# Mixture of experts in blocks of tokens: the incomplete block of an expert as its last item instead of its first

## What is computed

```python
logits = (xt @ w_router + b_router).astype(jnp.float32)
top_val, top_idx = lax.top_k(logits, TOP_K)          # TOP_K = 4, 32 experts
...
def expert_block(args):                              # blocks of 128 tokens of one expert
    xblk, e = args
    gate = xblk @ w_gate[e] + b_gate[e]
    up = xblk @ w_up[e] + b_up[e]
    gate = jnp.minimum(gate, SWIGLU_LIMIT)
    up = jnp.clip(up, -SWIGLU_LIMIT, SWIGLU_LIMIT)
    h = (up + 1.0) * gate * jax.nn.sigmoid(SWIGLU_ALPHA * gate)
    return h @ w_down[e] + b_down[e]
...
y = segment_sum(yb * row_w[:, None], row_tok)        # weighted sum over a token's four experts
```

## Time and profile before

| | us |
|---|---|
| median of three runs | 2398.84 (2397.83 to 2398.97) |
| the profiled execution | 2394.5 |
| its span, first to last instruction | 2392.6 |
| TensorE busy in the span | 2221.9 |
| start of the first G | 807.22 |
| end of the last D | 2345.9 |

### The profile page before, as it was taken

The page is one execution under the profiler, slowest core; times in us unless marked ns, Lnnn a source line. Parts: engine busy times, 40 slices in busy tenths (PEclk is TensorE's granted clock), DMA queues, the critical chain, the costliest instruction groups (busy, mean ns, idle before and its releaser), DMA issues.

```text
span 2392.6 us, 57077 instructions
## 1 busy us (share of the span) xinstructions
PE 2221.9 (93%) x21767; PEld 1176.8 (49%) x21768; DVE 1043.4 (44%) x1664; ACT 668.5 (28%) x1414; POOL 376.6 (16%) x491
## 2 busy tenths in 40 slices
PE   5999999998996599999999999999998999999982
PEld 3485765867454244545445454444443444444441
DVE  4154547445346344434434443443353444433334
ACT  5111222233344332222322222322232222222222
POOL 5000000000014212111111121111122112211111
PEclk9999999999997699999999999999999999999996
DMA  9112011126205294967979788888887897888864
GB/s 302 35 36 72 26 33 48 31 67 246 93 36 202 90 373 127 360 211 279 338 250 344 251 313 314 287 305 287 286 328 272 303 340 271 309 291 337 322 216 157
DMA packets 187702, 525.54 MB, mean 220 GB/s; under 512 B 20330, under 2 KB 68066, under 8 KB 187490
## 3 DMA queue, kind: packets, MB, share of 16 engines
q1 hardware_dynamic: 133874, 338.86, 37.7%
q10 hardware_dynamic: 36240, 134.29, 14.4%
q0 software_dynamic: 17536, 51.69, 9.6%
HBM read 486.21 MB, written 38.57 MB: 219 GB/s over the span
## 4 chain that ended last, share of the span: by engine, by line
PE 85%; DMA 6%; DVE 4%; issue 1%; ACT 1%; POOL 1%; ACTq 0%; SPq 0%; POOLq 0%; DVEq 0%
PE ps L1753 40%; PE ps L1786 19%; PE ps L1536 6%; PE ps L1637 5%; PE ps L1532 5%; DMA w_gu_e<-in_w_up_dram 4%; PE ps L1542 2%; PE ps L1593 2%; PE ps L1539 2%; PE ps L1615 1%; PE ps L1656 1%; PE ps L1508 1%; DMA w_down_e<-in_w_down_dram 1%; DVE box L1107 0%; DVE y_all L1460 0%
## 5 line engine op out<-in xcount | busy, mean ns | idle before, releaser
L1753 PE MATMUL ps<-w_gu_e,xT 128*32 128x512 f32 x9216 | 1007.7, 595 | 34.3 <-DVEq L1418 16.6
L1753 PEld LDWEIGHTS ps<-w_gu_e,xT 128*32 128x32 f32 x9216 | 355.9, 110 | 667.4 <-issue 667.1
L1786 PE MATMUL ps<-w_down_e,hT 128*32 128x256 f32 x9216 | 508.7, 380 | 13.4 <-ACT yrow L932 8.4
L1786 PEld LDWEIGHTS ps<-w_down_e,hT 128*32 128x32 f32 x9216 | 351.3, 110 | 181.8 <-issue 40.8
L1383 DVE STREAM_TRANSPOSE gu_t<-ps 128x1024 f32<-128x1024 f32 x94 | 111.9, 1229 | 639.4 <-PE ps L1753 639.4
L914 ACT ACTIVATE xT<-xr,fm 128x128 f32<-128x128 f32 x392 | 184.1, 490 | 569.0 <-PE ps L1753 544.6
L1369 DVE TENSOR_SCALAR yrow<-ps,slot_tab 32x256 f32<-32x256 f32 x376 | 181.3, 482 | 259.0 <-PE ps L1786 167.9
L932 ACT ACTIVATE yrow<-ps,slot_tab 32x256 f32<-32x256 f32 x384 | 179.4, 467 | 352.2 <-issue 235.9
L655 POOL DMA_INDIRECT xg<-xn_rows,idx_g x196 | 197.4, 1007 | 85.4 <-issue 47.6
L649 POOL TENSOR_TENSOR idx_g<-slot_tab,base_row 128x4 int32<-128x4 int32 x49 | 9.2, 189 | 1101.6 <-DVE xr L1405 1087.5
L1536 PE MATMUL ps<-hxT,w_ring 128*128 128x512 f32 (+1 forms) x384 | 142.5, 529 | 3.7 <-ACT hxT L802 3.7
(11 more groups left out here) (301 smaller groups left out, 1515.2 us busy)
## 6 DMA issues: line engine op xcount, KB each, us to landing
w_gu_e<-in_w_gate_dram SPq DMA_DIRECT2D x256, 512.0 KB, 10.7
w_gu_e<-in_w_up_dram SPq DMA_DIRECT2D x256, 512.0 KB, 11.6
w_down_e<-in_w_down_dram ACTq DMA_DIRECT2D x124, 1024.0 KB, 9.2
w_ring<-in_w_ada_dram SPq DMA_DIRECT2D x17, 1024.0 KB, 5.2
w_ring<-in_w_in_dram SPq DMA_DIRECT2D x20, 512.0 KB, 5.2
w_first<-in_w_ada_dram SPq DMA_DIRECT2D x7, 1024.0 KB, 12.2
x_all<-in_x_dram SPq DMA_DIRECT2D x2, 2048.0 KB, 10.6
w_out<-in_w_out_dram SPq DMA_DIRECT2D x8, 512.0 KB, 8.6
```

The source lines that it names most:

```text
L1753: last = T.matmul(ps[j * GROUP:(j + 1) * GROUP, g, :].rearrange("p (w b f) -> p w b f", w=2, f=GROUP), xT[:, k, g * GROUP:(g + 1) * GROUP] ...
L1786: last = T.matmul(ps[j * GROUP:(j + 1) * GROUP, 4 + g // 2, g % 2 * QUARTER:(g % 2 + 1) * QUARTER], hT[:, g, k, :], w_dn[:, k, j * QUARTER ...
```

## The change

Item j of an expert is now block j, and so its last item is the incomplete one. The mark `first_it[:, 0]` is set where the item's number plus one equals the number of blocks; column 0 of `of_it` stays as it is; the number of empty groups counts for the marked item only, as before.

```diff
             link(V.tensor_scalar(of_it[:, 0:1], of_it[:, 0:1], -1.0, item, ALU.mult, ALU.add))
-            link(V.tensor_scalar(first_it[:, 0:1], of_it[:, 0:1], 0.0, None, ALU.is_equal))
-            link(V.tensor_tensor(of_it[:, 1:3], of_it[:, 1:3], first_it[:, 0:1].to_broadcast([P, 2]), ALU.mult))
-            link(V.scalar_tensor_tensor(out=of_it[:, 0:1], in0=of_it[:, 0:1], scalar=-1.0, in1=of_it[:, 1:2],
-                                        op0=ALU.add, op1=ALU.add))
+            link(V.scalar_tensor_tensor(out=first_it[:, 0:1], in0=of_it[:, 0:1], scalar=1.0, in1=of_it[:, 1:2], op0=ALU.add,
+                                        op1=ALU.is_equal))
+            link(V.tensor_tensor(of_it[:, 2:3], of_it[:, 2:3], first_it[:, 0:1], ALU.mult))
             link(V.tensor_scalar(tab_it[:, 1:2], of_it[:, 0:1], float(GROUPS), None, ALU.mult))
```

## The result

The changed kernel takes 2447.84 us (median of four runs, 2445.02 to 2449.64), the one before 2398.34 in the runs beside it (four, 2396.50 to 2398.97). The ratio is 1.0208, with a 95% interval of 1.0195 to 1.0221: 49.5 us slower, where +39.8 had been forecast; the time lies within the range. The profiled execution took 2447.94 us, its span is 2446.2, 53.6 more than the span of before, which had been 4.3 us under its own median.

A forecast was written before the change was run, and what follows sets the result against it. TensorE was taken as the bound, busy 2221.9 of 2392.6 us, with only its waits able to move. 47.6 - 6.6 - 1 - 0.2 = +39.8 on 2398.84 gave 2438.6 us; the 8-in-10 range was 2415 to 2457.

The forecast's parts named there:

- (2): From a small expert to a big one: last w_gu chunk late for the full first item, 47.6 us in eleven places.
- t = 3, D of two groups, five times: Small expert's single item of three groups, then a two-group down pass: 3.75 us wait each, 18.7 us.
- t = 4, D of one, three times: Small expert's single item of four groups, then a one-group down pass: 5.2 us wait each, 15.6 us.
- t = 2, D of two, ahead of [4 4]: Small expert's single item of two groups, then a two-group down pass: one wait of 2.3 us.
- E: As a rival: nothing moves, within 0.2%, chance 0.05; in times like E + 6.2: end of a last item's gate-up pass.
- t = 2 ahead of [4 4 2]: Small expert's single item of two groups, then a one-group down pass: computed 9.4 us wait, taken as 7.5.
- p = 1 behind t = 3: One-group incomplete block of a big expert, behind a small expert's three-group item: one wait of 3.5 us.
- (1): From a big expert to a small one: waits of together 6.6 us go, and the starved gate-up pass loses 1 us.
- (3): Small parts: w_dn arrives in time by about 1 us, four scaled-row waits stay, the shorter table saves 0.2 us.
- B (w_gu keeps its pace): Rival: w_dn gets onto the engines no earlier than before, so 19 us of waits stay: about 2410 us, chance 0.08.
- C (the two queues served in turn): Rival: engines serve SP's w_gu before ACT's w_dn, so only the first place waits, 3 us: 2389 us, chance 0.05.
- D (output rows): Rival: down passes wait for the sum into y_rows, five places costing up to 5 us more: 2460 us, chance 0.08.

The follow-up runs named there:

- e7: Changed kernel plus three unused matmuls before the eighth chunk of each pass over groups 2 and 3, filling the wait: 2458.6 us, one run.
- e1: Changed kernel, but ACT issues a small expert's w_dn only after the eighth w_gu chunk in flight has landed: 2387.11 us (0.9957 of before); repeated, 2386.12 us (0.9954).
- e6: Changed kernel, but ACT issues a small expert's w_dn only after the fifth w_gu chunk in flight has landed: 2412.26 us, 1.0058 of before.
- e2: Changed kernel, but an incomplete block of one group stays the first item and only longer ones come last: 2424.87 us, 1.0116 of before.
- b1: Kernel before, old item order, with a small expert's w_dn issued only after the eighth w_gu chunk has landed: 2419.55 us, 1.0088 of before.

## Why the prediction was right, and what it missed

**(2), the waits that decide.** They stand where forecast and are near their sizes (us, from the rows of the timeline, like the two pieces above):

| the full G stands behind | forecast | measured |
|---|---|---|
| t = 3, D of two groups, five times | 18.7 | 3.56, 3.08, 2.55, 3.29, 3.11: 15.6 |
| t = 4, D of one, three times | 15.6 | 1.16 + 3.37, 1.54 + 3.17, 2.08 + 3.36: 14.7 |
| t = 3, D of one | 3.5 | 2.29 + 3.36: 5.65 |
| t = 2, D of two, ahead of [4 4] | 2.3 | 2.85 |
| t = 2, D of one, ahead of [4 4 2] | 7.5 | 1.65 + 3.25: 4.9 |
| sum | 47.6 | 43.7 |

The working behind them held in its steps. The timeline of ACT behind E = 1601.01, the sigmoid and the four issues of w_dn:

```profile
1606.84 1.06 ACT L919 ACTIVATE sig_t<-gu_t 128x1024 f32<-128x1024 f32 x1 [4.97 <-DVE gu_t L1389]
1607.20 2.21 ACTq L954 DMA_DIRECT2D w_down_e<-in_w_down_dram  x4
```

The transfer of the last w_gu chunk, issued between 1601.6 and 1602.1 (KB, us to landing):

```profile
w_gu_e<-in_w_up_dram SPq DMA_DIRECT2D x1, 512.0 KB, 20.8
```

The issue stands at E + 6.2, as said. The chunk lands at E + 21.7, against 22.7 in the sum; at 1403.88, where PE begins on it at E + 22.92, the sum is right. Due was E + 19.2, and x112 ends at E + 19.3. The queues in 1603 to 1610 and 1611 to 1620 (packets, MB, share of time; q1 is SP's, q10 ACT's):

```profile
q1 hardware_dynamic: 730, 2.67, 93.7%
...
q10 hardware_dynamic: 490, 1.94, 53.7%
q1 hardware_dynamic: 483, 1.74, 48.8%
```

From 1611, E + 10, ACT's queue has half of the engines, as in the earlier trace rows. In these 9 us both move 3.68 MB, 409 GB/s. The Trainium skill ("DMA: Bandwidth & Descriptors", Specifications) gives a limit of about 358 GB/s for a core; in this trace, of a kernel that runs on one core alone, two queues together moved more than that, as one queue did in the earlier trace rows.

Of the terms that were mis-sized, t = 2 ahead of [4 4 2] was taken at 7.5 for its late landing and measured 4.9, and p = 1 behind t = 3 was 2.2 too low, since I used its own early landing there (E + 16.3) and not the usual one.

**(1), what goes.** The waits ahead of the items of three groups behind [4 2] are gone, all of the 4.9 us, and so are the one of 0.58 behind [1 4] and the one for w_down. The starved G behind [4 1] has 0.69 + 1.50 + 1.46 = 3.65 us left of 5.67; I took off 1 and it was 2.0.

**(3)** held: D waits for nothing new. The four short waits ahead of D behind a one-group G are still four, 4.9 us (the row `<- issue` above).

**The missing term.** The forecast says that PE's own work stays the same and its busy time near 2222, and it has no term for the clock. It is 2245.1: 17.4 us more in G and D. That step of the prediction failed. In nine of the eleven places the x144 behind the wait take longer than 15.66 us: 18.37 once, 17.35 seven times, 17.10 once, 16.0 us too many in all. In the other two they do not, as here:

```profile
1526.47 15.66 PE L1752 MATMUL ps<-w_gu_e,xT 128*32 128x512 f32 x144 [3.08 <-DMA w_gu_e<-in_w_up_dram]
```

The trace of before had this price, and the prediction did not read it. On PE, the G behind a wait near the start, and the rest of the starved G of the earlier trace rows:

```profile
820.29 29.37 PE L1753 MATMUL ps<-w_gu_e,xT 128*32 128x512 f32 x256 [3.70 <-issue]
...
1842.83 17.65 PE L1753 MATMUL ps<-w_gu_e,xT 128*32 128x512 f32 x136 [1.43 <-DMA w_gu_e<-in_w_up_dram]
```

The stretch at the start of the second, in the columns given above:

```profile
1842.83:1846.00 3.17, 3.17 (x16) 0.88 (x20) 0.00 (x0) 0.00 (x0) 1.94 (x2) 0.50 0.14 41
```

The x256 take 1.7 us more than 27.67, and the x136 2.85 more than the 14.80 of the earlier trace rows, at a granted clock of 0.50. At 1.7 us for each of eleven waits, the term would have been an estimated 19 us against the 16.0 measured. The 16.5 us of G are thus a net figure: 16.0 behind the eleven waits, 1.7 more behind the waits at the start, and 2.9 less in the starved G, whose x136 now take 14.80; the small rest is not resolved.

e7 shows the cause, with the order kept and the waits filled; e1 shows that it goes with the waits, too. Without this term the sum of the waits was 5.0 us too high (w_up waits +36.2, where +41.2 follow from the sum: 3.9 in the table, 1.0 at the starved G, the rest rounding); so in the experts' part 40.0 - 5.0 + 17.4 is 52.4, against the 52.1 of the traces (40.0 is the forecast without the table's 0.2). That the time fell within the range is in part luck, because these two errors have opposite signs.

**The rivals.** B (w_gu keeps its pace): ACT's queue is moving by 1611, as early as its issues allow, out. C (the two queues served in turn): 53.7 to 48.8, out. D (output rows): the only wait for yrow is one of 7.0 us, which the kernel before has as well, and the four short ones do not grow; out. E: out by the time itself. e1 is the cleanest word on all of them: with w_dn out of the way the new order loses nothing.

What stays open: why two of eleven waits of the same length did not lower the clock, and why e6 spreads over 12 us. In e2 three of five such waits (2.61, 3.30 and 2.25 us) did not lower it either, and those of 4.11 and 3.67 did, with 18.44 and 17.35 us for the x144. So the price per wait is an average over places, 1.5 us here, and not a figure for one wait.

## What to carry to other kernels

When two loads share the DMA engines, ask which of them is needed first, and what decides when the other is issued: here a shorter piece of work let the less urgent 4 MB in 2.8 us earlier, and that delayed the urgent load by about as much (e6 held them back for 2.4 us of it, and the waits behind a D of two groups shrank by 2.2 to 3.1). A reordering that only moves work is best tried together with the wait that holds the less urgent load back, since each may be worth nothing, or be a loss, without the other (b1 +0.9%, the change +2.1%, both -0.5%). Look, too, at what else stands in the program of the engine that is made to wait: in b1 it was ACT's scaling of rows that came late, and not the load. And a wait of some 3 us on TensorE should be priced with the slow matmuls behind it: here 43.7 us of such waits cost another 16.

## What the runs showed of the hardware that I had not expected

- A wait of 2.55 us (1622.87) or 2.85 us, with PE busy all the time before, was followed by a granted clock of 0.50; a wait of 3.08 us (1526.47) was not. Where it happened, the next 15.66 us of work took 1.4 to 2.7 us longer. In the kernel before, four waits of 1.2 to 1.5 us with 1.06 us of work between them were followed by a granted clock of 0.50 as well (1842.83).
- A loop body on PE that grew by one copied pass was fetched again as it ran: 33 instruction packets became 394, 0.54 MB became 6.46, and the kernel took 665 us longer; for 514 us PE stood still with nothing in the profile to wait for. Three more matmuls in the existing pass (e7) left the count at 33.
- From the issue on ACT's queue to its first packets it took 3.3 to 3.8 us with SP's queue full (1607.20 to between 1610.5 and 1611), no longer than before the change.
